# Two attentions of a transformer's last layer run as one sequence of 24 softmax steps, with the projections dealt out over it

## The chip, the cores and the metric

The kernel runs on one core of a Trainium2 chip. The metric is the device time of one execution in microseconds (us), as a median over runs. The engines are TensorE (PE in the rows; PEld is its weight load), VectorE (DVE), ScalarE (ACT), GpSimd (POOL, used only at the start) and SyncE (SP, which issues the loads of the weights). Each engine works through its own list of instructions in order, and the engines wait for each other by semaphores.

## The reference

The program computes four layers over 256 tokens of width 1024 in float32. The change touches the mixer of the last layer. There, with `h` the normalised input, `q` comes in 8 heads of 128 and `qm` in 4 heads of 128:

```python
proj = h @ b_w_q[j]                                  # 1024 x 1536
q  = proj[..., :1024].reshape(b, s, 8, 128)
qm = proj[..., 1024:].reshape(b, s, 4, 128)
# forgetting attention: causal, keys and values made before the layer's first feed-forward
logits = einsum('bqhd,bkhd->bhqk', q_blk, k) * scale + c_blk[..., :, None] - logf_cum[:, :, None, :]
p = softmax(where(causal, logits, NEG_INF));  y_tok = einsum('bhqk,bkhd->bqhd', p, v)
# memory attention: 256 memory positions, no mask
p = softmax(einsum('bshd,bmhd->bhsm', qm, mk) * dh ** -0.5);  y_mem = einsum('bhsm,bmhd->bshd', p, mv)
x = x + concatenate([y_tok, y_mem], -1) @ b_w_out[j]  # 1536 x 1024
```

## The kernel before

**Units.** The weights stream from HBM in units of 1 MB through a ring of three slots. A unit is loaded by SyncE into `raw`, ScalarE rounds it into `w_hi` (`split`, L1122), and VectorE makes the remainder `w_lo = raw - w_hi` (L1717). An *up* unit gives 256 columns of a projection from `normed` (L588 to L590: 8 pieces of k, each of 6 matmuls: two halves times hi by hi, hi by lo, lo by hi). A *down* unit takes 256 rows of an output projection and adds into all 1024 columns, which lie in PSUM banks 0 to 3 (L637 to L640: 8 column blocks `m`, each of 6 matmuls). When TensorE has finished a unit (`su_done`), ScalarE and then VectorE split the next contents of that slot; the slot's next load waits for VectorE's part (`lo_split`). The input of a down unit is prepared by `feed` (ScalarE L1220, VectorE L1827), which TensorE awaits as `hid_ready`.

**A softmax step** treats one head `h` and one half `a` of the queries (128 rows). Step n runs over the engines like this:
- TensorE, `scores(n)` (L830 for the last attention, called "fox"; L832 for the memory attention, "mem1"), issued two steps ahead: at the head of step n stands `scores(n+2)`. Then come `between(n)`, `values(n-1)` (L853) and `turn(n)` (L839), the transposes of the probabilities, which wait for `probs_ready(n)`.
- VectorE: `shift(n+1)` (the maximum, L2000; in fox an addition of the decays and the mask before it, L1994), `normalise(n)` (L2008, L2013), `between(n)`.
- ScalarE: `exps(n)` (L1318 or L1321), on odd n `copy_out` of a head (L1333), `copy_turned(n-1)` (L1328), `between(n)`.

`between` is where other work is woven in by hand. No planner orders it: the order of every engine is the order of this code.

**The stage around the change.** After the norm, TensorE does up units 0 and 1 (the memory queries), transposes the values, and does up unit 2. Then comes mem1, 8 steps, with up units 3 to 5 in halves (4 pieces of k a step) woven into its steps 0 to 5 (`B_WOVEN = 3`); its steps 6 and 7 have nothing between. Then TensorE waits until the last queries are evacuated and the last head is copied out, and fox begins, 16 steps, with down units 0 to 3 and a quarter of down unit 4 in quarters (two blocks `m`, 12 matmuls) woven in, three quarters ahead of step 1 by the table `FOX_DOWNS`. In fox a finished unit's slot is split whole, within the step that follows its last quarter, first by ScalarE and then by VectorE, in both queues ahead of the next step's softmax work. The rest of down unit 4, down unit 5 and the feed-forward follow. The mem1 scores use banks 0, 1 and 2 in turn and await nothing; the fox scores use banks 4 and 5 and await the `shift` of two steps before. Keys of a fox step are 128 for a = 0 and 256 for a = 1.

## Time and profile before

| what | us |
|---|---|
| median of 3 runs (1910.40 to 1911.62) | 1910.89 |
| the profiled execution's own time | 1911.35 |
| its span, first to last instruction | 1909.6 |
| TensorE busy in the span | 1830.5 (96%) |
| VectorE busy | 1353.2 (71%) |
| ScalarE busy | 1008.9 (53%) |
| the stretch from mem1's first scores to fox's last values | 1622.4 to 1700.4 |

Busy time of TensorE counts matmuls with their modelled ends, so back-to-back matmuls overlap in the rows; the time that a matmul costs is the distance from its start to the next start. In rows of the order of time, the figure in brackets is how long the engine was idle before, and what released it. The mean granted TensorE clock was 0.984 of full speed.

### The profile page before, as it was taken

How to read it: one execution, taken by the hardware profiler on the slowest of the kernel's cores; microseconds unless marked ns; L12 is line 12 of the kernel's file. 1: busy time of each engine (PE TensorE's matmuls, PEld its weight loads, DVE VectorE, ACT ScalarE, POOL GpSimd, SP SyncE). 2: the span in 40 equal slices, each digit the busy share in tenths (PEclk: the TensorE clock that was granted, in tenths of full speed). 3: DMA queues.
4: the chain of work that ended last, by engine and by line, in shares of the span. 5: the costliest groups of instructions: out<-in, count | busy, mean ns of one | idle time of the engine just before them, and what ended most of it. 6: DMA issues, size and time to landing. Idle time of an engine off the chain costs nothing.

```text
span 1909.6 us, 32527 instructions
## 1 busy us (share of the span) xinstructions
PE 1830.5 (96%) x12825; PEld 1700.1 (89%) x12825; DVE 1353.2 (71%) x1705; ACT 1008.9 (53%) x1205; POOL 5.3 (0%) x34
## 2 busy tenths in 40 slices
PE   6989899999999999999999999999999999899998
PEld 6988798998888889989999999999989999889997
DVE  5968668888788678886667666666756666666665
ACT  5744455566656555565445435444544445465443
POOL 1000000000000000000000000000000000000000
PEclk9999999999999999999999999999999999999999
DMA  6632155555533345556555554655645555336552
GB/s 187 189 121 89 50 172 176 177 197 182 172 116 133 112 167 172 187 166 208 178 179 175 172 177 155 198 177 176 198 134 203 180 188 167 121 101 209 176 178 85
DMA packets 237941, 310.18 MB, mean 162 GB/s; under 512 B 8227, under 2 KB 213801, under 8 KB 237865
## 3 DMA queue, kind: packets, MB, share of 16 engines
q1 hardware_dynamic: 236520, 308.03, 48.7%
q10 hardware_dynamic: 1344, 1.09, 0.2%
q8 instruction: 54, 0.88, 0.2%
q14 instruction: 23, 0.18, 0.0%
HBM read 308.04 MB, written 1.06 MB: 162 GB/s over the span
## 4 chain that ended last, share of the span: by engine, by line
PE 85%; DVE 8%; ACT 4%; issue 3%; DMA 0%; SPq 0%; DVEq 0%; ACTq 0%
PE ps L609 23%; PE ps L611 12%; PE ps L637 9%; PE ps L639 9%; PE ps L640 9%; PE ps L588 6%; PE ps L590 6%; PE ps L589 6%; DVE weights_lo L1717 2%; ACT weights_hi L1122 2%; PE ps L853 1%; DVE scratch L1767 1%; DVE scratch L1763 1%; ACT scratch L1245 1%; PE ps L756 1%
## 5 line engine op out<-in xcount | busy, mean ns | idle before, releaser
L1717 DVE TENSOR_TENSOR weights_lo<-raw_weights,weights_hi 128x2048 fp32r<-128x2048 f32 x290 | 663.9, 2290 | 260.6 <-ACT weights_hi L1122 260.1
L609 PE MATMUL ps<-normed,weights_hi 128*128 128x512 f32 x2112 | 749.3, 399 | 2.5 <-DVE normed L1807 2.4
L1122 ACT ACTIVATE weights_hi<-raw_weights 128x2048 fp32r<-128x2048 f32 x290 | 552.0, 1906 | 207.2 <-PE ps L590 84.5
L611 PE MATMUL ps<-normed,weights_lo 128*128 128x256 f32 x2112 | 593.1, 281 | 0.0
L609 PEld LDWEIGHTS ps<-normed,weights_hi 128*128 128x128 f32 x2112 | 396.9, 188 | 97.8 <-DVE weights_lo L1717 2.7
L637 PE MATMUL ps<-down_in_hi,weights_hi 128*128 128x256 f32 x1440 | 415.6, 289 | 18.9 <-DVE down_in_lo L1827 7.0
L639 PE MATMUL ps<-down_in_lo,weights_hi 128*128 128x256 f32 x1440 | 412.2, 286 | 0.0
L640 PE MATMUL ps<-down_in_hi,weights_lo 128*128 128x256 f32 x1440 | 411.9, 286 | 0.0
L611 PEld LDWEIGHTS ps<-normed,weights_lo 128*128 128x128 f32 x2112 | 399.2, 189 | 0.1
L588 PE MATMUL ps<-normed,weights_hi 128*128 128x256 f32 x1088 | 321.8, 296 | 10.7 <-DVE normed L1807 7.3
L589 PE MATMUL ps<-normed,weights_hi 128*128 128x256 f32 x1088 | 310.4, 285 | 0.0
L590 PE MATMUL ps<-normed,weights_lo 128*128 128x256 f32 x1088 | 310.4, 285 | 0.0
L637 PEld LDWEIGHTS ps<-down_in_hi,weights_hi 128*128 128x128 f32 x1440 | 281.2, 195 | 24.0 <-issue 13.7
L639 PEld LDWEIGHTS ps<-down_in_lo,weights_hi 128*128 128x128 f32 x1440 | 281.3, 195 | 0.2
L640 PEld LDWEIGHTS ps<-down_in_hi,weights_lo 128*128 128x128 f32 x1440 | 281.1, 195 | 0.0
L588 PEld LDWEIGHTS ps<-normed,weights_hi 128*128 128x128 f32 x1088 | 211.4, 194 | 15.3 <-issue 10.9
L589 PEld LDWEIGHTS ps<-normed,weights_hi 128*128 128x128 f32 x1088 | 211.4, 194 | 3.3 <-issue 2.6
L590 PEld LDWEIGHTS ps<-normed,weights_lo 128*128 128x128 f32 x1088 | 211.2, 194 | 0.0
L1191 ACT ACTIVATE scratch<-ps 128x512 f32<-128x512 f32 x132 | 78.3, 594 | 176.7 <-PE ps L611 176.7
L1763 DVE TENSOR_TENSOR scratch<-ps,scratch 128x512 f32<-128x512 f32 x132 | 90.7, 687 | 50.7 <-ACT scratch L1191 50.7
L1864 DVE SCALAR_TENSOR_TENSOR scratch<-scratch,vectors 128x254 f32<-128x254 f32 (+1 forms) x176 | 73.4, 479 | 60.9 <-ACT scratch L1245 60.9
L1245 ACT ACTIVATE scratch<-scratch,vectors 128x256 f32<-128x256 f32 x88 | 48.1, 594 | 116.8 <-DVE scratch L1767 116.8
(248 smaller groups left out, 1310.0 us busy)
## 6 DMA issues: line engine op xcount, KB each, us to landing
raw_weights<-in_ffn_w_gate_up_dram SPq DMA_DIRECT2D x88, 1024.0 KB, 5.1
raw_weights<-in_ffn_up_w_dram SPq DMA_DIRECT2D x44, 1024.0 KB, 5.1
raw_weights<-in_ffn_w_down_dram SPq DMA_DIRECT2D x44, 1024.0 KB, 5.0
raw_weights<-in_ffn_down_w_dram SPq DMA_DIRECT2D x22, 1024.0 KB, 4.9
raw_weights<-in_ssd_in_w_dram SPq DMA_DIRECT2D x20, 1024.0 KB, 5.3
raw_weights<-in_a_w_in_dram SPq DMA_DIRECT2D x14, 1024.0 KB, 5.1
raw_weights<-in_attn_in_w_dram SPq DMA_DIRECT2D x12, 1024.0 KB, 5.1
raw_weights<-in_ssd_out_w_dram SPq DMA_DIRECT2D x8, 1024.0 KB, 4.9
```

Source lines behind the costliest of these rows:

```text
L588: mm(o, hi, h_hi[:, k, :], start=(k == 0 and a == 0), stop=False, skip_group_check=True)
L589: mm(o, hi, h_lo[:, k, :], start=False, stop=False, skip_group_check=True)
L590: last = mm(o, lo, h_hi[:, k, :], start=False, stop=(k == DK - 1), skip_group_check=True)
L609: mm(ps[:, b + a, :], wh[:, k, a * P:(a + 1) * P], h[:, k, :, :].rearrange("p c t -> p (c t)"), start=(k == 0), stop=False, skip_group_che ...
L611: last = mm(ps[:, b + a, 0:T], wl[:, k, a * P:(a + 1) * P], h_hi[:, k, :], start=False, stop=(k == DK - 1), skip_group_check=True)
L637: mm(o, hi, act_hi[:, s, k, :], start=(first and k == 0 and m % 2 == 0), stop=False, skip_group_check=True)
L639: mm(o, hi, act_lo[:, s, k, :], start=False, stop=False, skip_group_check=True)
L640: ins = mm(o, lo, act_hi[:, s, k, :], start=False, stop=(k == 1), skip_group_check=True)
L1122: f(w_hi[:, s, :], raw[:, s, :], ACT.Copy).then_inc(hi_split.sem, hi_split.plus())
L1191: f(f_in[:, w, :, :], low_part(b), ACT.Copy).then_inc(low_copied.sem, low_copied.plus())
L1717: tt(w_lo[:, s, :], raw[:, s, :], f32(w_hi[:, s, :]), ALU.subtract).then_inc(lo_split.sem, lo_split.plus())
L1763: tt(f_in[:, w, :, :], main_part(b), f_in[:, w, :, :], ALU.add).then_inc(step.sem, step.plus())
```

## The change

Mem1 and fox become one sequence of 24 steps (8 and 16) without a wait between them. Only PSUM banks 4 and 5 hold scores now, in both kinds, bank 6 the transposes, bank 7 the values. So the scores of step n+2 await `exps` of step n where step n is of mem1 (it reads the bank directly), and `shift(n)` where it is of fox. The up units lie in banks 0, 1, 2, 1, 2, 0. Up units 3 to 5 are dealt out over steps 0 to 10 in pieces of 3, 3 and then 2 k a step. Down units 0 to 2 and the first quarter of down unit 3 are dealt out over steps 11 to 23, a quarter a step, with the blocks in reverse order; three quarters of unit 3 and units 4 and 5 follow the sequence. The order of the inputs is heads of mem1 first, then fox (`MIXED_ORDER`). A slot freed by the unit that ends in step t is split in halves of 1024 columns: ScalarE in steps t+1 and t+2, VectorE in steps t+3 and t+4. The two key masks of each half move from steps 0 to 3 to steps 1 and 4.

```diff
-B_WOVEN = 3
-FOX_PIECES = [(i, 2 * q) for i in range(5) for q in range(4)]
-FOX_DOWNS = {0: FOX_PIECES[0:2], **{t: FOX_PIECES[t + 1:t + 2] for t in range(1, 16)}}
-FOX_FED = {5: 0, 9: 1, 13: 2}
+MIXED_ORDER = (4, 5, 0, 1, 2, 3)
+JOINT_UPS = (3, 3, 2, 2, 2, 2, 2, 2, 2, 2, 2)
+JOINT_ENDS = {-1: ("up", 2), 2: ("up", 3), 6: ("up", 4), 10: ("up", 5), 14: ("down", 0), 18: ("down", 1), 22: ("down", 2)}
+JOINT_FED = {6: 0, 10: 1, 14: 2, 18: 3, 22: 4, 24: 5}
+JOINT_UP_BANKS = (0, 1, 2, 1, 2, 0)
+JOINT_KEYS = {1: (0, 1), 4: (2, 3)}
...
+        def score_bank(kind, n):
+            return 4 + n % 2 if joint(kind) else n % 3
...
                 def scores(n):
+                    kind, h, a = steps[n]
+                    b, nk = score_bank(kind, n), keys_of(kind, a)
+                    if joint(kind) and n >= 2:
+                        if steps[n - 2][0] == "fox":
+                            pe.wait_ge(shifted.sem, shifted.value(n - 1))
+                        else:
+                            pe.wait_ge(exps_done.sem, exps_done.value(n - 1))
...
-            softmax_attention("mem1", woven(B_WOVEN))
-            pe.wait_ge(evacuated.sem, evacuated.value())
-            pe.wait_ge(out_read.sem, out_read.value(1))
...
+            def joint_step(t):
+                if t < len(JOINT_UPS):
+                    query_parts(t)
+                else:
+                    quarter = t - len(JOINT_UPS)
+                    out_quarter(quarter // 4, quarter % 4)
+
+            softmax_attention(("mem1", "fox"), joint_step)
+            for q in range(1, 4):
+                out_quarter(3, q)
+            down_unit()
             down_unit(last=True)
...
+            def joint_step(t):
+                if t - 1 in JOINT_ENDS:
+                    act.wait_ge(su_done.sem, su_done.next())
+                    split_part(0)
+                if t - 2 in JOINT_ENDS:
+                    split_part(1)
+                    if JOINT_ENDS[t - 2][0] == "up":
+                        act.wait_ge(evacuated.sem, evacuated.next())
+                if t in JOINT_FED:
+                    act.wait_ge(out_read.sem, out_read.value())
+                    feed(mixed, MIXED_ORDER[JOINT_FED[t]], (out_slot + JOINT_FED[t]) % RING)
...
+            def split_part(part):
+                s, half = slot[0], slice(1024 * part, 1024 * part + 1024)
+                if part == 0:
+                    dve.wait_ge(hi_split.sem, hi_split.next())
+                ins = tt(w_lo[:, s, half], raw[:, s, half], f32(w_hi[:, s, half]), ALU.subtract)
...
+            def joint_step(t):   
+                if t - 1 in JOINT_ENDS:
+                    dve.wait_ge(su_done.sem, su_done.next())
+                    kind, j = JOINT_ENDS[t - 1]
+                    if kind == "up":
+                        last_queries(j - 2, None)
+                if t in JOINT_FED:
+                    feed(mixed, MIXED_ORDER[JOINT_FED[t]], (out_slot + JOINT_FED[t]) % RING)
+                for part in (0, 1):
+                    if t - 3 - part in JOINT_ENDS:
+                        split_part(part)
+                if t == 1:
                     dve.wait_ge(keys_staged.sem, keys_staged.next(2))
...
+                for i in JOINT_KEYS.get(t, ()):
+                    mask_keys(i)
```

In TensorE's list before, between the last woven up unit and the first down unit, stand these rows (L853 values, L839 turns, L832 scores of mem1, L830 scores of fox, L637 the first matmul of a down unit):

```order
L590 MATMUL ps<-normed,weights_lo 128x256
L853 MATMUL ps<-scratch,mem_v 128x128 x2
L839 MATMUL ps<-ident,scratch 128x128 x2
L853 MATMUL ps<-scratch,mem_v 128x128 x2
L839 MATMUL ps<-ident,scratch 128x128 x2
L853 MATMUL ps<-scratch,mem_v 128x128 x2
L839 MATMUL ps<-ident,scratch 128x128 x2
L853 MATMUL ps<-scratch,mem_v 128x128 x2
L830 MATMUL ps<-proj 128x128
L830 MATMUL ps<-proj 128x256
L830 MATMUL ps<-proj 128x128
L637 MATMUL ps<-down_in_hi,weights_hi 128x256
```

Four values, three turns and three scores stand there with no unit between them. In the changed list the same place, the end of the memory heads, reads so (L869 values, L855 turns, L845 scores of fox, L602 to L604 the matmuls of an up unit, of which 12 stand in each step):

```order
L869 MATMUL ps<-scratch,mem_v 128x128 x2
L855 MATMUL ps<-ident,scratch 128x128 x2
L845 MATMUL ps<-proj 128x128
L602 MATMUL ps<-normed,weights_hi 128x256
L603 MATMUL ps<-normed,weights_hi 128x256
L604 MATMUL ps<-normed,weights_lo 128x256
...
L869 MATMUL ps<-scratch,mem_v 128x128 x2
L855 MATMUL ps<-ident,scratch 128x128 x2
L845 MATMUL ps<-proj 128x256
L602 MATMUL ps<-normed,weights_hi 128x256
```

Two pieces of an up unit now stand in every step there, and the first fox scores are in front of such a piece.

In VectorE's list of fox before, from one `shift` to the next but one (L1994 and L2000 `shift`, L2008 and L2013 `normalise`, L1717 the split of a slot):

```order
L1994 SCALAR_TENSOR_TENSOR scratch<-ps,columns,scratch 128x128
L2000 TENSOR_REDUCE scratch<-scratch 128x1
L2008 RECIPROCAL scratch<-scratch 128x1
L2013 TENSOR_SCALAR scratch<-scratch 128x256
L1717 TENSOR_TENSOR weights_lo<-raw_weights,weights_hi 128x2048
L1994 SCALAR_TENSOR_TENSOR scratch<-ps,columns,mem_k 128x256
L2000 TENSOR_REDUCE scratch<-scratch 128x1
L2008 RECIPROCAL scratch<-scratch 128x1
L2013 TENSOR_SCALAR scratch<-scratch 128x128
L1994 SCALAR_TENSOR_TENSOR scratch<-ps,columns,scratch 128x128
```

The whole split of 2048 columns stands ahead of the shift of a 256-key step. Now, around step 10, the first with both a `feed` and a half split (L1885 the feed, L1766 a half split, L2052 and L2058 `shift`, L2066 and L2071 `normalise`, L1836 the evacuation of the last queries):

```order
L2071 TENSOR_SCALAR scratch<-scratch 128x128
L1885 TENSOR_TENSOR down_in_lo<-proj,down_in_hi 128x512
L1766 TENSOR_TENSOR weights_lo<-raw_weights,weights_hi 128x1024
L2052 SCALAR_TENSOR_TENSOR scratch<-ps,columns,scratch 128x128
L2058 TENSOR_REDUCE scratch<-scratch 128x1
L2066 RECIPROCAL scratch<-scratch 128x1
L2071 TENSOR_SCALAR scratch<-scratch 128x256
L1836 SCALAR_TENSOR_TENSOR proj<-ps,rstd 128x512
L2052 SCALAR_TENSOR_TENSOR scratch<-ps,columns,mem_k 128x256
```

The feed and a half split of 1024 columns stand ahead of the shift of a 128-key step and the `normalise` of the 256-key step before it. The other half stands three steps later.

## Rows read from the trace of the kernel before

**Rows 1.** The page: busy time, share of the span and instructions of each engine.

```profile
PE 1830.5 (96%) x12825; PEld 1700.1 (89%) x12825; DVE 1353.2 (71%) x1705; ACT 1008.9 (53%) x1205; POOL 5.3 (0%) x34
```

**Rows 2.** Stretches: length, busy PE, PEld, DVE, ACT, POOL (instructions), PE clock, DMA share, GB/s.

```profile
1622.40:1646.00 23.60, 23.60 (x188) 23.18 (x188) 17.54 (x32) 11.17 (x24) 0.00 (x0) 1.00 0.50 169
1646.00:1656.00 10.00, 5.54 (x31) 3.97 (x29) 5.78 (x10) 5.60 (x12) 0.00 (x0) 0.82 0.48 178
1656.00:1659.30 3.30, 3.30 (x18) 3.30 (x17) 1.61 (x7) 0.60 (x2) 0.00 (x0) 0.51 0.23 89
1681.90:1692.70 10.80, 9.23 (x74) 8.94 (x74) 7.26 (x19) 5.83 (x17) 0.00 (x0) 1.00 0.29 96
1622.40:1700.40 78.00, 68.08 (x518) 64.94 (x518) 49.38 (x109) 39.03 (x96) 0.00 (x0) 0.96 0.35 119
```

**Rows 3.** Order of time, TensorE, one mem1 step: start, length, instruction, count.

```profile
1626.84 0.60 PE L832 MATMUL ps<-mem_k,proj 128*128 128x256 f32 x2
...
1630.13 0.61 PE L853 MATMUL ps<-scratch,mem_v 128*128 128x128 f32 x4
...
1630.58 0.38 PE L839 MATMUL ps<-ident,scratch 128*128 128x128 f32 x2
...
1630.80 0.60 PE L832 MATMUL ps<-mem_k,proj 128*128 128x256 f32 x2
```

**Rows 4.** Order of time, TensorE, from mem1 to fox.

```profile
1646.03 0.61 PE L853 MATMUL ps<-scratch,mem_v 128*128 128x128 f32 x4
...
1651.66 0.71 PE L853 MATMUL ps<-scratch,mem_v 128*128 128x128 f32 x4 [0.53 <-ACT scratch L1328]
...
1655.49 0.80 PE L830 MATMUL ps<-proj 128*128 128x128 f32 x2 [0.93 <-DVE scratch L2000]
...
1655.94 0.56 PE L637 MATMUL ps<-down_in_hi,weights_hi 128*128 128x256 f32 x1
...
1659.27 0.28 PE L637 MATMUL ps<-down_in_hi,weights_hi 128*128 128x256 f32 x1
```

**Rows 5.** Order of time, TensorE, in and after fox.

```profile
1668.93 0.60 PE L853 MATMUL ps<-scratch 128*128 128x128 f32 x4
...
1671.11 0.33 PE L839 MATMUL ps<-ident,scratch 128*128 128x128 f32 x1 [1.57 <-DVE scratch L2013]
...
1681.91 0.33 PE L839 MATMUL ps<-ident,scratch 128*128 128x128 f32 x1 [1.57 <-DVE scratch L2013]
...
1699.94 0.71 PE L853 MATMUL ps<-scratch 128*128 128x128 f32 x4 [0.73 <-ACT scratch L1328]
```

**Rows 6.** Order of time, ScalarE and VectorE, a whole split in fox.

```profile
1665.50 1.91 ACT L1122 ACTIVATE weights_hi<-raw_weights 128x2048 fp32r<-128x2048 f32 x1
...
1667.52 2.29 DVE L1717 TENSOR_TENSOR weights_lo<-raw_weights,weights_hi 128x2048 fp32r<-128x2048 f32 x1 [3.10 <-ACT weights_hi L1122]
```

**Rows 7.** Order of time, the three engines, the first mem1 steps.

```profile
1622.45 1.46 PE L832 MATMUL ps<-mem_k,proj 128*128 128x256 f32 x6
...
1623.08 0.86 DVE L2000 TENSOR_REDUCE scratch<-ps 128x1 f32<-128x256 f32 x2 [0.87 <-PE ps L832]
...
1623.91 0.19 ACT L1321 ACTIVATION_READ_ACCUMULATOR scratch<-ps,scratch 128x1 f32 x1
```

**Rows 8.** Groups by line and form, over the kernel: 1024 columns wide.

```profile
L1793 DVE TENSOR_TENSOR scratch<-scratch 128x1024 f32<-128x1024 f32 x11 | 13.4, 1221 | 1.3 <-ACT scratch L1204 1.2
...
L1421 ACT ACTIVATE proj<-proj 128x1024 f32<-128x1024 f32 x4 | 4.2, 1054 | 0.7 <-DVE proj L2156 0.7
```

**Rows 9.** Order of time, ScalarE and VectorE, a feed; then a shift and normalise.

```profile
1671.64 0.62 ACT L1220 ACTIVATE down_in_hi<-proj 128x512 fp32r<-128x512 f32 x1
...
1672.30 0.69 DVE L1827 TENSOR_TENSOR down_in_lo<-proj,down_in_hi 128x512 fp32r<-128x512 f32 x1 [0.21 <-ACT down_in_hi L1220]
...
1674.15 0.35 DVE L1994 SCALAR_TENSOR_TENSOR scratch<-ps,columns,scratch 128x128 f32<-128x128 f32 x1
...
1674.92 0.35 DVE L2013 TENSOR_SCALAR scratch<-scratch 128x256 f32<-128x256 f32 x1
```

More of the change, by code:

```diff
@@ L328, in attention, with joint, softmax_steps @@
                     "mem0": (MEM_HEADS, 24, 36, P ** -0.5), "mem1": (MEM_HEADS, 24, 36, P ** -0.5)}[kind]
+        def joint(kind):
+            return kind in ("mem1", "fox")
         def turned_bank(kind):
-            return 6 if kind == "fox" else 3
+            return 6 if joint(kind) else 3
+        def score_bank(kind, n):
+            return 4 + n % 2 if joint(kind) else n % 3
+        def softmax_steps(kinds):
+            return [(kind, h, a) for kind in kinds for h in range(attention(kind)[0]) for a in range(TH)]
         def keys_of(kind, a):
@@ L622, in woven, with down_unit @@
                 return step
-            def down_unit(first=False, last=False, ms=range(DK)):
+            def down_unit(first=False, last=False, ms=range(DK), begin=True, end=True):
                 s = slot[0]
-                if ms[0] == 0:
+                if begin:
                     pe.wait_ge(lo_split.sem, lo_split.next())
@@ L1117, in _ @@
             slot, unit = [0], [0]
+            def split_part(part):
+                s, half = slot[0], slice(1024 * part, 1024 * part + 1024)
+                if part == 0:
+                    act.wait_ge(landed[s].sem, landed[s].next())
+                ins = f(w_hi[:, s, half], raw[:, s, half], ACT.Copy)
+                if part:
+                    ins.then_inc(hi_split.sem, hi_split.plus())
+                    unit[0] += 1
+                    slot[0] = (s + 1) % RING
             def split(s):
@@ L2022, in softmax_attention @@
                 shift(0)
[L2023 to L2024 removed]
+                for n in range(len(steps)):
+                    if n + 1 < len(steps):
                         shift(n + 1)
@@ L2027, in softmax_attention @@
                     between(n)
-                for n in range(2 * n_heads, 2 * n_heads + 3):
+                for n in range(len(steps), len(steps) + 3):
                     between(n)
@@ L2376, in _ @@
-            softmax_attention("mem1", mem_step)
-            turned.n += 4
-            dve.wait_ge(out_read.sem, out_read.next(MEM_HEADS))
-            mixed = proj[:, 28:40, :]
-            for j in range(2):
-                feed(mixed, 4 + j, (slot[0] + j) % RING)
-            def fox_step(t):
-                if 0 < t <= 15 and FOX_DOWNS[t - 1][-1][1] == DK - 2:
-                    dve.wait_ge(su_done.sem, su_done.next())
-                    split_next()
-                if t in FOX_FED:
-                    feed(mixed, FOX_FED[t], (slot[0] + 1) % RING)
@@ L2390, in _, with mask_keys @@
-            softmax_attention("fox", fox_step)
-            dve.wait_ge(out_read.sem, out_read.next(FOX_HEADS))
-            feed(mixed, 3, (slot[0] + 1) % RING)
+            memory_queries = queries_to_proj(24, JOINT_UP_BANKS)
+            last_queries = queries_to_proj(16, JOINT_UP_BANKS[2:])
+            units(2, memory_queries, evacuated=1)
+            mixed, out_slot = proj[:, 28:40, :], (slot[0] + 1) % RING
+            def mask_keys(i):
+                rows_of = key_rows[i // 2]
+                if i % 2:
+                    tt(rows_of[:, :, P:T], rows_of[:, :, P:T], rows(causal_mask[:, P:T], 4),
+                       ALU.add).then_inc(step.sem, step.plus())
+                else:
+                    tt(first_rows[:, 2 * i:2 * i + 4, :], rows_of[:, :, 0:P], rows(causal_mask[:, P:T], 4),
+                       ALU.add).then_inc(step.sem, step.plus())
+                dve.wait_ge(step.sem, step.value())
```

163 lines of the change are left out of this document (77 added, 86 removed).

## The prediction

> **What bounds the kernel now.** I read the page first, for the shares: TensorE is busy in 96% of the span [rows 1], so a change can only pay where TensorE stands still or runs slow. Then I took the busy time in stretches of the part that the change touches, 1622.4 to 1700.4: 78.0 us, of which TensorE shows 68.1 busy and VectorE 49.4 [rows 2]. The clean part of mem1 has no gap. The 10 us after it hold only 5.5 us of TensorE work, the next 3.3 us run at a granted clock of 0.51 (the 1.2 GHz level), and in fox a period of 10.8 us holds 9.2 us of work [rows 2]. Last I went to the rows in order of time, to price each loss by the distance between starts.
>
> What a step costs when nothing waits: a mem1 step of before runs from 1626.84 to 1630.80, 3.96 us. Values take 1630.13 to 1630.58, 0.45; the turn 0.22 to 1630.80; so scores with 24 matmuls of projection take 3.29, and at 0.12 a matmul (2.88) the scores are 0.41 [rows 3]. A piece of 128 keys takes half of each.
>
> **What the change removes.** Four losses of TensorE in that stretch.
>
> (a) The seam between the attentions. From the values at 1646.03 to the first down matmul at 1655.94 are 9.91 us [rows 4]. The work in it is four values (1.80), three turns (0.66) and scores of 128, 256 and 128 keys (0.21 + 0.41 + 0.21): 3.3 us. 6.6 us are waits: chains from engine to engine with nothing woven in. In the changed list that work has two pieces of an up unit in every step (1.44 us). Removed: 6.6, if the chains fit under the cover, which is checked below.
>
> (b) The slow clock behind the seam. From 1655.94 to 1659.27 15 matmuls start, at 0.213 us each where 0.12 is normal [rows 4], at the clock of 0.51 [rows 2]. 3.33 less 15 x 0.12 and 0.1 for the entry from float32 work: 1.4 us, and it goes with the idle time before it.
>
> (c) Three waits of a turn in fox. The values begin at 1668.93 and cost 0.45; the turn starts at 1671.11 [rows 5]: 1.73 us. The same row stands at 1681.91, and a third 10.8 us on, at 1692.72: 5.2 us together. Their cause is a whole split in line: ScalarE's 1.91 us at 1665.50 and VectorE's 2.29 at 1667.52 run one after the other [rows 6], and the exponentials and shifts queue behind each.
>
> (d) The last values of the sequence start 0.73 us late behind the copy [rows 5]; the copy waited for a whole split of ScalarE. With half of it in front, the wait should be that of a chain with ScalarE free, as at 1651.66: 0.53 [rows 4]. Removed: 0.2.
>
> **What it adds.** (e) The scores of step 2 now wait for the exponentials of step 0. Before, six instructions of scores ran through from 1622.45 [rows 7]. Now two scores end at 1622.45 + 0.82 = 1623.27 and the third waits for the maximum (from 1623.08) and the exponential, whose accumulator is read at 1623.91 + 0.19 = 1624.10 [rows 7]. With the signal, TensorE goes on at about 1624.12: 0.85 us lost, with nothing before it to cover. The same kind of wait stands ahead of every later score, and is covered there as follows.
>
> (f) The halves. A 1024-column instruction takes 1.22 on VectorE and 1.05 on ScalarE [rows 8]; two of them against one whole, 2.29 and 1.91 [rows 6]: 0.15 and 0.2 more a split, seven splits: 1.1 and 1.4 us. They lie beside TensorE unless they are on a chain. The Trainium skill, "VectorE: DVE Perf Modes", section on the TRN2 errata, says that operations from SBUF pay a fixed extra per instruction, so that many small tiles pay it each time. The rows agree that it is there; whether it is paid in time depends on the chain.
>
> (g) Moves. Four quarters of a down unit (4 x 1.43 us) leave the sequence and run behind it, as much work as before. Queries, masks, feeds and splits are as many as before. ScalarE's feed and the loads of SyncE move earlier or later by steps; the tightest load is that of the slot that is freed last, and it has more than 10 us of down units ahead of its use, where a step moved it by one. I cost it at nothing.
>
> **Do the chains fit?** Without waits a mem1 step with two pieces is 0.41 + 1.44 + 0.45 + 0.22 = 2.52 us, and four fox steps are 10.80 - 1.73 = 9.07 us [rows 5], 2.2 for a = 0 and 2.3 for a = 1. All the work of VectorE in the stretch is 49.4 us [rows 2], plus 1.1 for the halves, in a stretch that shrinks to 78.0 - 12.2 less the four quarters, some 60 us, in which about 5 of that work (two splits) moves behind it: three quarters full. So it does not bind by its sum, but in one place by its order.
>
> Mem1, scores(n+2): at the head of step n TensorE wants exps(n). ScalarE may begin step n-1's copy when the turn is done; copy, half a split (1.05) and the exponential with its read take 0.2 + 0.3 + 0.95 + 0.65 = 2.1 us from the head of step n-1; the step lasts 2.52. It fits by 0.4. Values(n-1) need the copy only at 1.85 us: it fits by more than 1.
>
> Fox: the tight place is the step with a feed and a half split, t = 10, 14, 18, 22. Let F be TensorE's start of step t. Before, the turn of a 128-key step started at 1671.11, so F was 1671.22, and the feed began at 1671.64 [rows 9], F + 0.42; behind a 256-key step the copy is longer by an estimated 0.1: F + 0.52. VectorE's feed follows 0.66 later and takes 0.62 to the next start [rows 9]: F + 1.8. The half split takes 1.13 of the 1.22 to the next start: F + 2.93. Then stand shift(t+2) and normalise(t+1): 1674.15 to 1674.92 + 0.35, 1.12 us [rows 9]: F + 4.05. TensorE reaches turn(t+1) after a step of 2.2, and 0.41 + 1.43 + 0.22: F + 4.26. It fits by 0.2 us. That is less than I can read from the rows, so I put 0.3 us in all for those four places. With a whole split there it would not fit by 0.9. Everything else has half a microsecond or more.
>
> **The sum.** Removed 6.6 + 1.4 + 5.2 + 0.2 = 13.4; added 0.85 + 0.3 = 1.15; net 12.2. The profiled execution took 1911.35 us (its span 1909.6 and 1.75 around it), 0.46 above the median of the runs. 1911.35 - 12.2 = 1899.1; against the median, 1910.89 - 12.2 = 1898.7. I predict 1898.7.
>
> Bounds. The unknowns are the new waits. From below: no wait at all, also not at (e), gives 13.4, 1897.5; I add 1 us for what my starts cannot see, 1896.5. From above: the four tight places may each wait as long as a whole half split on VectorE, 1.2 us [rows 8], 4.9 in all; 1903.3.
>
> **The rivals.**
>
> Feed-bound fox. VectorE waits for ScalarE's feed, and the feed for the copy behind the turn, so a late turn makes the next one late. For it: the 0.2 us of margin, and the 0.21 us that VectorE already waits for the feed [rows 9]. Against it: it comes once in four steps, and the other three have slack to catch up. It gives 0.5 to 1.2 us at four places and the same, once, at step 6: 2.5 to 6 us, 1901 to 1904.5.
>
> Every fixed cost counts. By that page's rule on small tiles, if each half stood on the chain, (f) would cost its full 2.5 us: 1901.2. The rows speak against it: VectorE works 7.3 of the 10.8 us of a period [rows 2] and its half split stands three steps after the unit's end.
>
> The clock falls inside the sequence. The seam shows the price: 3.3 us at 0.51 cost 1.4 us. For it: the gap of 0.85 at the start and alternating small work. Against it: in fox before, three gaps of 1.57 us left the clock at 1.00 [rows 2, 5]. Two such falls would give 2.8 us, 1901.5. The Trainium skill, "TensorE: Matmul & The Clock Gate", section on PSUM-queue cycling, tells of a kernel whose small idles between groups of matmuls made the clock go back and forth; the rows of this stretch do not agree, with gaps and a clock of 1.00.
>
> Slower than before: two banks instead of three bind every step. The mechanism is the loop scores, maximum, exponential, scores over two steps. In the sequence a step may last (78.0 - 4 x 1.43) / 24 = 3.0 us before the time is as before, so the loop would have to take more than 6.0 us per two steps in all 24. Its parts are 0.6 from scores to maximum, 0.9 for a shift with its addition, 0.65 for the exponential, and, if both halves of a split and a feed always fell into it, 1.05 + 1.22 + 0.62: 5.0 us. For it: the waits are new and stand at the head of the step, ahead of the cover. At 6.5 us per loop the kernel is 6 us slower, 1917. It decides only if the rows' durations grow, and I see no reason.
>
> The change does nothing: the seam comes back behind the sequence, since the three quarters and two units run with idle partners. They run back to back before, too. 1910.9.
>
> **How the numbers follow.** Forecast (within 1.5 us of 1898.7) 0.62; feed-bound fox 0.18; fixed costs 0.06; clock 0.04; less than the forecast for reasons I do not see, but still faster, 0.03; no change 0.04; slower 0.03. The range 1896.3 to 1903.2 holds the first and most of the next three. About 0.2% (3.8 us) is what a measurement of this kernel can tell from no change. Faster by more than that 0.93, within it 0.04, slower 0.03.
>
> **What the profile after would show.** Right: from the last woven matmul of mem1 on, no gap between values and scores, a granted clock of 1.00 from the first to the last step, and one PE wait of about 0.85 us for ScalarE's exponential at the third scores. Steps of 2.5 us in mem1 with two pieces and four fox steps in 9.1 us. (c) is wrong if turns still wait for L2071; the place to look is turn 11, 15, 19, 23. (d) shows 0.5 before the last values. (a) is wrong if scores wait for the exponential in each mem1 step. If the stretch shrinks by 13 us and the time does not, the loss is in the feed-forward behind it, in its first three units.

## The result, and the profile after

| what | before | after |
|---|---|---|
| median of 3 runs | 1910.89 (1910.40 to 1911.62) | 1897.06 (1895.60 to 1897.52) |
| the profiled execution | 1911.35 | 1897.52 |
| its span | 1909.6 | 1895.6 |
| granted clock over the span | 0.984 | 0.987 |

The ratio of the runs is 0.992, with a 95% interval of 0.9903 to 0.9938: 11.8 to 18.5 us faster. Forecast were 1898.7 us, 12.2 us faster; measured are 13.8 by the medians.

First the page of the profile after, the line that answers to [rows 1]:

```profile
PE 1824.9 (96%) x12825; PEld 1697.4 (90%) x12825; DVE 1353.2 (71%) x1712; ACT 1008.5 (53%) x1212; POOL 5.3 (0%) x34
```

TensorE has as many instructions as before, VectorE and ScalarE have seven more each (the halves). To see where the time went, cut the execution at two rows of TensorE: the first memory scores, and the first wide matmul of the feed-forward behind the mixer. The rows of the profile after, in order of time (start, length, instruction; in brackets the idle time and its releaser):

```profile
1621.28 1.03 PE L847 MATMUL ps<-mem_k,proj 128*128 128x256 f32 x4
1622.99 0.70 PE L847 MATMUL ps<-mem_k,proj 128*128 128x256 f32 x2 [0.68 <-ACT scratch L1364]
...
1680.17 0.71 PE L869 MATMUL ps<-scratch 128*128 128x128 f32 x4 [0.47 <-ACT scratch L1372]
...
1696.54 0.40 PE L623 MATMUL ps<-normed,weights_hi 128*128 128x512 f32 x1
```

And the end of the same stretch in the profile of before; its beginning is 1622.45 [rows 7]:

```profile
1710.55 0.40 PE L609 MATMUL ps<-normed,weights_hi 128*128 128x512 f32 x1
```

| piece of the span | before | after | difference |
|---|---|---|---|
| start to first memory scores | 1622.45 | 1621.28 | -1.17 |
| the stretch (first memory scores to first wide matmul) | 88.10 | 75.26 | -12.84 |
| behind it | 199.05 | 199.06 | 0.0 |

The last row is the span less the two others, and the span is printed to 0.1 us: hundredths count there for nothing. The instructions of the first piece and of the last are the same in both kernels, in the same order on TensorE, VectorE and ScalarE. The change made the stretch 12.84 us shorter; the 1.17 us in front are another matter, for the experiments. In the stretch the profile after has just the two waits of TensorE shown above. The view of stretches (length, busy PE, PEld, DVE, ACT, POOL, then PE clock, DMA share, GB/s), after, answers to [rows 2]:

```profile
1621.30:1696.50 75.20, 74.05 (x602) 72.63 (x601) 55.24 (x124) 44.91 (x112) 0.00 (x0) 1.00 0.40 136
```

and of before, the same work:

```profile
1622.40:1710.50 88.10, 78.18 (x602) 75.04 (x602) 54.91 (x117) 44.24 (x105) 0.00 (x0) 0.96 0.35 117
```

The granted clock is now 1.00 throughout, and busy TensorE fell too, by 4.1 us: the matmuls at the lower level are gone, and with the waits the modelled ends that stand ahead of them. A memory step, as [rows 3] had it, and four fox steps, as [rows 5] had them; after, order of time, TensorE:

```profile
1631.45 0.38 PE L855 MATMUL ps<-ident,scratch 128*128 128x128 f32 x2
...
1633.99 0.38 PE L855 MATMUL ps<-ident,scratch 128*128 128x128 f32 x2
...
1650.73 0.27 PE L855 MATMUL ps<-ident,scratch 128*128 128x128 f32 x1
...
1659.74 0.27 PE L855 MATMUL ps<-ident,scratch 128*128 128x128 f32 x1
...
1668.76 0.27 PE L855 MATMUL ps<-ident,scratch 128*128 128x128 f32 x1
```

2.54 us for the memory step with two pieces (forecast 2.52), 9.01 and 9.02 for four fox steps (forecast 9.07).

The tight place, step 10, in all three engines, after. TensorE's step starts with L845 at F = 1648.63:

```profile
1648.63 0.39 PE L845 MATMUL ps<-proj 128*128 128x128 f32 x2
...
1649.11 0.62 ACT L1262 ACTIVATE down_in_hi<-proj 128x512 fp32r<-128x512 f32 x1
...
1649.77 0.69 DVE L1885 TENSOR_TENSOR down_in_lo<-proj,down_in_hi 128x512 fp32r<-128x512 f32 x1 [0.67 <-ACT down_in_hi L1262]
...
1650.38 1.22 DVE L1766 TENSOR_TENSOR weights_lo<-raw_weights,weights_hi 128x1024 fp32r<-128x1024 f32 x1
...
1651.51 0.34 DVE L2052 SCALAR_TENSOR_TENSOR scratch<-ps,columns,scratch 128x128 f32<-128x128 f32 x1
...
1652.28 0.35 DVE L2071 TENSOR_SCALAR scratch<-scratch 128x256 f32<-128x256 f32 x1
...
1652.92 0.38 PE L855 MATMUL ps<-ident,scratch 128*128 128x128 f32 x2
```

The `normalise` (L2071) is done at 1652.63, F + 4.00 (forecast F + 4.05), and the turn that needs it starts at F + 4.29 (forecast F + 4.26), without a wait: a margin of 0.29 us. (The half split in this step is the second of its slot. The first stands one step earlier, at 1646.64, and not three steps later.) This is how a fit is read: not from the busy share, but from the end of the last instruction of the chain to the start of what would wait for it.

### The profile page after: what moved, and what is told of

Read it like the earlier page. It is cut to its first block, busy times and chain, and to the rows that moved or that the text cites. A ratio compares the mean times of both kernels' runs of the same rounds, so it can differ in the third digit from the quotient of the medians.

```text
span 1895.6 us, 32539 instructions
## 1 busy us (share of the span) xinstructions
PE 1824.9 (96%) x12825; PEld 1697.4 (90%) x12825; DVE 1353.2 (71%) x1712; ACT 1008.5 (53%) x1212; POOL 5.3 (0%) x34
## 4 chain that ended last, share of the span: by engine, by line
PE 86%; DVE 8%; ACT 3%; issue 3%; DMA 0%; SPq 0%; DVEq 0%; ACTq 0%
PE ps L623 23%; PE ps L625 12%; PE ps L651 9%; PE ps L653 9%; PE ps L654 9%; PE ps L602 6%; PE ps L604 6%; PE ps L603 6%; DVE weights_lo L1775 2%; ACT weights_hi L1164 1%; PE ps L869 1%; DVE scratch L1825 1%; DVE scratch L1821 1%; ACT scratch L1287 1%; PE ps L770 1%
## 5 line engine op out<-in xcount | busy, mean ns | idle before, releaser
L1775 DVE TENSOR_TENSOR weights_lo<-raw_weights,weights_hi 128x2048 fp32r<-128x2048 f32 x283 | 647.9, 2290 | 250.3 <-ACT weights_hi L1164 249.7
L1164 ACT ACTIVATE weights_hi<-raw_weights 128x2048 fp32r<-128x2048 f32 x283 | 538.5, 1905 | 208.7 <-DVE scratch L1825 84.3
L602 PE MATMUL ps<-normed,weights_hi 128*128 128x256 f32 x1088 | 322.2, 296 | 10.9 <-DVE normed L1865 7.2
L604 PE MATMUL ps<-normed,weights_lo 128*128 128x256 f32 x1088 | 310.4, 285 | 0.0
L602 PEld LDWEIGHTS ps<-normed,weights_hi 128*128 128x128 f32 x1088 | 211.3, 194 | 15.3 <-issue 10.6
L604 PEld LDWEIGHTS ps<-normed,weights_lo 128*128 128x128 f32 x1088 | 211.2, 194 | 0.0
```

The costliest lines, as they stand in the source:

```text
L602: mm(o, hi, h_hi[:, k, :], start=(k == 0 and a == 0), stop=False, skip_group_check=True)
L604: last = mm(o, lo, h_hi[:, k, :], start=False, stop=(k == DK - 1), skip_group_check=True)
L1164: f(w_hi[:, s, :], raw[:, s, :], ACT.Copy).then_inc(hi_split.sem, hi_split.plus())
L1775: tt(w_lo[:, s, :], raw[:, s, :], f32(w_hi[:, s, :]), ALU.subtract).then_inc(lo_split.sem, lo_split.plus())
```

## The experiments

Each run is measured against the kernel before on the same chip. "Stretch" is cut as above; TensorE's waits are all those in the stretch, from the order of time.

**The kernel once more, five executions.** No edit.

> The changed kernel once more, against the kernel before, on another occasion. Theory (chance outside the change): the stretch from the first scores of the memory attention to the first matmul of the last feed-forward takes 75.3 us again (88.1 before) and what follows it 199.1, both within 0.2; the arrival at the stretch, where all instructions are those of before, moves by 1 us or more from one execution to the next with the places at which the granted clock is low. Median difference 12.8 us, give or take 1. Rival (something systematic beyond the stretch): the stretch is 12.8 us shorter, but the medians stand 14 to 15 us apart again, and the arrival is about 1.2 us earlier again.

Measured: median 1898.44 us of 5 (1896.82 to 1900.71), before 1911.88 of 11 (1908.59 to 1915.68); ratio 0.9932, interval 0.9918 to 0.9946, that is 13.0 us (10.3 to 15.7). The profile: arrival at the first memory scores 1621.86, stretch 75.26, behind it 199.08. The stretch repeats to the hundredth; the arrival does not.

**Is the arrival chance?** The kernel before once more, one profile.

> The kernel before, unchanged, one profile. Theory (the granted clock ahead of the stretch differs from one execution to the next, in the same instructions): the first memory scores start anywhere between 1620 and 1624.5 us and not at 1622.45 again, while the stretch is 88.1 and the rest to the end of the span 199.05, each within 0.1 us. Rival (the change itself, through the loads, moves the arrival earlier): the arrival is later here than in every profile of the changed kernels, 1622.4 or more, and the stretch or the rest may differ by more than 0.3.

Measured: arrival 1622.28, stretch 88.10, behind it 199.12; the time is 1911.18. Alone it does not decide, since 1622.28 is close to 1622.45. All profiles together say more: in kernels that are the same up to the first memory scores the arrival lies from 1620.17 to 1624.22 (table below), on both sides of before. The mean of eleven profiles of changed kernels is 1622.08, that of two of before 1622.37. Where the spread arises, the start of the same whole split on ScalarE shows in four of them (numbered in order of time):

| profile | 26th | 75th | 87th | 111th | 124th | arrival |
|---|---|---|---|---|---|---|
| before | 236.2 | 539.5 | 647.9 | 793.4 | 873.5 | 1622.45 |
| after | 235.7 | 538.9 | 645.3 | 790.6 | 871.5 | 1621.28 |
| third bank (below) | 234.1 | 537.4 | 645.8 | 791.2 | 871.3 | 1620.17 |
| whole with the feed (below) | 238.6 | 541.8 | 648.2 | 793.5 | 874.3 | 1624.22 |

From the 75th to the 87th two take 108.4 us and two 106.4; from the 111th to the 124th those with 108.4 take 80.1 and the others 80.8 or 80.9. The rows of the stretches there, before:

```profile
600.00:640.00 40.00, 33.92 (x227) 30.68 (x226) 23.22 (x46) 20.50 (x46) 0.00 (x0) 0.87 0.29 103
840.00:880.00 40.00, 37.58 (x252) 34.48 (x251) 31.58 (x38) 26.59 (x31) 0.00 (x0) 1.00 0.50 163
```

and after:

```profile
600.00:640.00 40.00, 33.74 (x244) 30.80 (x243) 24.92 (x46) 20.63 (x47) 0.00 (x0) 0.96 0.29 102
840.00:880.00 40.00, 37.91 (x238) 34.83 (x239) 30.90 (x35) 27.27 (x30) 0.00 (x0) 0.96 0.48 159
```

The third bank's profile has the clocks of before there (0.87, 1.00), the whole split with the feed those of after (0.96, 0.96), worth 2.0 and 0.8 us. These are not the only values: over all thirteen profiles the first window was granted 0.87 ten times, 0.91 once and 0.96 twice, the second 1.00 seven times, 0.96 four times and 0.91 twice, and the changed kernel has 0.96 and 0.96 in one of its two profiles, 0.87 and 1.00 in the other. The rest of the spread is there by the 26th split, 234.1 to 238.6; its cause was not read. So the arrival moves by itself, and no run ties the 1.17 us to the change; with two profiles of before, a shift of some tenths can't be told from none. Why a place is granted the lower level in one execution and not in the next, no run here shows.

**A third bank for the one scores that wait uncovered.** It undoes (e) alone.

```diff
-            return 4 + n % 2 if joint(kind) else n % 3
+            return (3 if n == 2 else 4 + n % 2) if joint(kind) else n % 3
-                    if joint(kind) and n >= 2:
+                    if joint(kind) and n >= 3:
```

> The third scores go to PSUM bank 3, which is free by then, and wait for nothing. Theory: the wait of TensorE for the exponential at the start goes, and nothing takes its place, so the stretch is 0.7 to 0.85 us shorter than 75.3, about 74.5. Rival (the wait only moves one step on, to the scores of step 3, as the exponential of step 1 queues behind half a split): less than 0.2 us.

Measured: stretch 74.32, 0.94 less; one execution, 1895.46 us. Only the wait of 0.47 before the last values is left. So (e) costs 0.94 us; the row shows 0.68 of it.

**A quarter of a down unit ahead of the last values.** It covers what (d) left.

```diff
-            softmax_attention(("mem1", "fox"), joint_step)
-            for q in range(1, 4):
+            softmax_attention(("mem1", "fox"), joint_step, before_last=lambda: out_quarter(3, 1))
+            for q in range(2, 4):
```

> The last values stand behind the next quarter of the down unit, not ahead of it. Theory: the wait of 0.47 us for the copy goes under 12 matmuls, the stretch is 0.5 us shorter, about 74.8. Rival: the last feed, which needs the last head copied out, comes 1.4 us later and holds up the last down unit: the stretch is as long or longer.

Measured: stretch 74.52, 0.74 less; one execution, 1895.92 us. The row showed 0.47. Again the wait costs a quarter of a microsecond more than its idle time. The rows say where it lies. First, idle time is counted from the modelled end of the matmul before, and that end is later than the next start has to be: in [rows 3] the turn at 1630.58 takes 0.38, to 1630.96, and the scores behind it start at 1630.80, 0.16 earlier. Second, the instruction behind a wait is longer itself: scores take 0.70 where they take 0.60 without a wait, values 0.71 for 0.61, a turn 0.33 for 0.27. So a wait costs its idle time and 0.26 us more ahead of scores or values, and 0.22 more ahead of a turn.

**Both.**

> Both edits (third scores in bank 3, last values behind a quarter). Theory: they add, since each takes away one wait of TensorE and leaves none: stretch 74.1 us (1.2 shorter), no wait of TensorE left in the sequence; the median 1.2 us under that of the changed kernel, which the rounds can hardly tell. Rival: one of them is only moved, 0.5 to 0.8.

Measured: stretch 73.57, 1.69 less, the sum of the two. Median 1897.37 of 6 (1896.09 to 1897.82, and one execution of 3581.61; 1897.00 without that one), before 1911.88; ratio 0.9924, interval 0.991 to 0.9937. So it was executed again, on another chip:

> The kernel with bank 3 for the scores of step 2 and a down quarter ahead of the last values, measured once more. Theory that what lies outside the stretch is chance: the stretch from the first scores to the first wide matmul of the feed-forward is 73.6 us (within 0.1) and TensorE waits nowhere in it; the median lies between 1896.0 and 1898.5 us, 13.5 to 15.5 below the kernel before of the same runs; no execution of 3582 us comes back. Rival, that the long execution belongs to this kernel: it comes again at least once in the six.

Measured: median 1896.23 of 5 (1895.20 to 1898.82), before 1911.2 of 9 (1909.29 to 1915.06); ratio 0.9923, interval 0.9909 to 0.9937: 14.7 us. Stretch 73.58. No long execution came back; where the 3581.61 came from stays open (its granted clock was 1.0). In this kernel TensorE is busy without a gap; two of its stretches, as the others:

```profile
1650.00:1660.00 10.00, 10.00 (x83) 9.85 (x82) 8.93 (x21) 6.59 (x20) 0.00 (x0) 1.00 0.31 107
1660.00:1670.00 10.00, 10.00 (x85) 9.90 (x84) 8.26 (x24) 7.01 (x19) 0.00 (x0) 1.00 0.32 107
```

That gives the measure for everything else: 73.57 us is the stretch with no wait at all. (The brackets alone don't prove it, as the last experiment shows. The distances from start to start do: none is longer than the same pair of instructions takes in the other steps of its kind.) The interval of the medians overlaps that of the changed kernel. That this kernel is the faster of the two rests on the stretch, which repeats to 0.01 us, and not on the medians.

**The seam, with the projection left in mem1.** Up units 3 to 5 in steps 0 to 5 as before, nothing between in steps 6 to 10; one sequence all the same.

```diff
-JOINT_UPS = (3, 3, 2, 2, 2, 2, 2, 2, 2, 2, 2)
+JOINT_UPS = (4, 4, 4, 4, 4, 4, 0, 0, 0, 0, 0)
-JOINT_ENDS = {-1: ("up", 2), 2: ("up", 3), 6: ("up", 4), 10: ("up", 5), ...}
+JOINT_ENDS = {-1: ("up", 2), 1: ("up", 3), 3: ("up", 4), 5: ("up", 5), ...}
```

> The up units stand in steps 0 to 5, 4 pieces a step, as before; steps 6 to 10 of the joint sequence have nothing between. Theory (uncovered steps are what the seam cost, not the two waits that separated the attentions): such a step takes 1.4 us where its work is 1.1 (memory) or 0.75 (last attention), more where a half split stands in the chain: 4 to 7 us in all, and if the granted clock falls in it, 1.4 more: stretch 79 to 84 us. Rival (the separating waits were the cost): under 2 us longer.

Measured: median 1907.37 of 10 (1904.93 to 1911.21), before 1910.31 of 13 (1908.94 to 1914.87); ratio 0.9981, interval 0.9971 to 0.9991. Stretch 84.92, 9.66 longer than in the changed kernel. TensorE's waits in the bare steps, order of time (a sixth, of 0.25, is at 1654.40):

```profile
1649.12 0.71 PE L869 MATMUL ps<-scratch,mem_v 128*128 128x128 f32 x4 [0.25 <-ACT scratch L1372]
...
1651.04 0.70 PE L845 MATMUL ps<-proj 128*128 128x256 f32 x2 [0.99 <-ACT scratch L1364]
...
1653.49 0.44 PE L855 MATMUL ps<-ident,scratch 128*128 128x128 f32 x2 [1.12 <-DVE scratch L2071]
...
1655.86 0.33 PE L855 MATMUL ps<-ident,scratch 128*128 128x128 f32 x1 [0.75 <-DVE scratch L2071]
...
1658.09 0.69 PE L855 MATMUL ps<-ident,scratch 128*128 128x128 f32 x2 [0.98 <-DVE scratch L2071]
```

and its stretches:

```profile
1650.00:1660.00 10.00, 5.84 (x27) 4.05 (x27) 9.14 (x20) 5.81 (x18) 0.00 (x0) 0.89 0.32 107
1660.00:1670.00 10.00, 10.00 (x65) 9.48 (x64) 5.53 (x20) 3.94 (x15) 0.00 (x0) 0.77 0.30 107
1670.00:1680.00 10.00, 10.00 (x85) 9.90 (x84) 7.02 (x19) 6.91 (x20) 0.00 (x0) 1.00 0.01 2
```

Joining the two attentions gives nothing by itself. The stretch is 3.18 us shorter than before (84.92 for 88.10), but no turn waits behind the bare steps here, so that the 5.37 us of (c) and 0.26 of (d) (both measured below) are gained and 0.94 of (e) is paid, 4.69 in all: the bare seam costs 1.5 us more than the old one with its separating waits. Cover in every step gives the 9.66. In the bare steps VectorE binds (9.14 of 10 us): the steps are short, and four half splits of 1.22 us fall into steps 6 to 9, one in each. No run has bare steps without these splits, so what part of the 9.66 us is theirs and what part the missing cover's, is not shown. The granted clock falls in the last bare steps (0.50 from 1658 to 1662) and is 0.77 over these ten us, much as at the old seam [rows 2, 4], and 1.00 again in the next ten. The 9.66 us are more than the 5.4 to 8.4 that I had given it: I had priced chains of waits, and not that VectorE's half splits fall into the bare steps.

**A whole split in line, in fox.** It undoes (c) for the down units.

```diff
 # ScalarE
-                    split_part(0)
-                if t - 2 in JOINT_ENDS:
+                    if JOINT_ENDS[t - 1][0] == "up":
+                        split_part(0)
+                    else:
+                        split_next()
+                if t - 2 in JOINT_ENDS and JOINT_ENDS[t - 2][0] == "up":
...
 # VectorE, under "if t - 1 in JOINT_ENDS"
+                    else:
+                        split_next()
...
-                    if t - 3 - part in JOINT_ENDS:
+                    if t - 3 - part in JOINT_ENDS and JOINT_ENDS[t - 3 - part][0] == "up":
```

> For the down units the two engines split whole in step t+1, one behind the other, as the last attention did before; the up units' slots in halves as in the changed kernel. Theory: the waits of 1.7 us come back at the turns of steps 16 and 20; the one behind step 22 has only the last turn behind it, and the last values then wait 0.3 to 2 us more: the stretch is 3.5 to 5.5 us longer, about 80. Rival (the waits of before came from the seam's rhythm and not from the serial split): under 1 us longer.

Measured: median 1901.99 of 4 (1900.54 to 1902.00), before 1910.31; ratio 0.9953, interval 0.9936 to 0.9969. Stretch 79.10, 3.84 longer. The old waits come back with their old length [rows 5]:

```profile
1666.78 0.33 PE L855 MATMUL ps<-ident,scratch 128*128 128x128 f32 x1 [1.57 <-DVE scratch L2075]
...
1677.59 0.33 PE L855 MATMUL ps<-ident,scratch 128*128 128x128 f32 x1 [1.57 <-DVE scratch L2075]
...
1684.81 0.71 PE L869 MATMUL ps<-scratch 128*128 128x128 f32 x4 [0.73 <-ACT scratch L1372]
```

The last wait is 0.26 longer than in the changed kernel (0.73 for 0.47), and 3.84 - 0.26 = 3.58 is 1.79 us for each of the other two.

**Halved, or only moved? A whole split with the feed.** VectorE's split stands whole at step t+4, the step of the feed.

```diff
-                for part in (0, 1):
-                    if t - 3 - part in JOINT_ENDS:
-                        split_part(part)
+                if t - 4 in JOINT_ENDS:
+                    split_next()
```

> VectorE splits a slot whole in step t+4 (the step that also has a feed); ScalarE still in halves. Theory (the tight place is the one with feed and split, margin 0.27 us in the changed kernel's trace): 1.07 us more of VectorE in front makes the turn of steps 11, 15 and 19 late by 0.8 us each, that of step 7 by 0.2; step 23 has no shift behind it and waits 0.2 at most: the stretch is 2.4 to 2.9 us longer, about 78. Rival (there is slack of a whole step, the halves buy nothing): under 0.5 us longer.

Measured: median 1902.98 of 4 (1901.24 to 1904.61), before 1910.31; ratio 0.9957, interval 0.9941 to 0.9974. Stretch 79.44, 4.18 longer, where I had expected 2.4 to 2.9. The tight place, all three engines, to be read beside step 10 above:

```profile
1663.76 2.28 DVE L1775 TENSOR_TENSOR weights_lo<-raw_weights,weights_hi 128x2048 fp32r<-128x2048 f32 x1
...
1665.97 0.34 DVE L2052 SCALAR_TENSOR_TENSOR scratch<-ps,columns,scratch 128x128 f32<-128x128 f32 x1
...
1666.73 0.35 DVE L2071 TENSOR_SCALAR scratch<-scratch 128x256 f32<-128x256 f32 x1
...
1667.14 0.44 PE L855 MATMUL ps<-ident,scratch 128*128 128x128 f32 x2 [0.67 <-DVE scratch L2071]
```

The same turn waits after each feed: 0.33 at 1647.34, 0.67 three times, and 0.74 at 1686.36, which I had put at 0.2 or less. 3.1 us idle at five places cost 4.18: 0.22 more for each, the price of a wait ahead of a turn.

**Whole, but one step earlier.** No halves at all: ScalarE whole in step t+1, VectorE whole in step t+3, where no feed stands.

```diff
-                    split_part(0)
+                    split_next()
...
-                for part in (0, 1):
-                    if t - 3 - part in JOINT_ENDS:
-                        split_part(part)
+                if t - 3 in JOINT_ENDS:
+                    split_next()
```

> No halves at all: ScalarE splits whole in step t+1, VectorE whole in step t+3, ahead of the feed step. Theory (the place of VectorE's split matters, not its halving): VectorE is done with it before the feed comes, and the turns in fox do not wait; ScalarE's whole split delays the exponential of step 4, for which the scores of step 6 wait, by 0.4 us: the stretch is 0 to 0.6 us longer than 75.3. Rival (halving is what took the waits of fox away): 1.5 us or more at each of four places, 81 us.

Measured: median 1898.89 of 4 (1898.64 to 1901.69), before 1910.31; ratio 0.9943, interval 0.9926 to 0.996. Stretch 76.03, 0.77 longer. No turn waits in fox. Two waits are new or longer, both for ScalarE, one at memory scores (0.25 + 0.26 = 0.51) and one before the last values (0.26 more):

```profile
1635.57 0.70 PE L847 MATMUL ps<-mem_k,proj 128*128 128x256 f32 x2 [0.25 <-ACT scratch L1364]
...
1681.89 0.71 PE L869 MATMUL ps<-scratch 128*128 128x128 f32 x4 [0.73 <-ACT scratch L1372]
```

**Whole splits in the kernel without waits.** Both edits of "both", and these.

> Bank 3 and the quarter ahead of the last values, and every slot split whole: ScalarE one step after the unit's end, VectorE three steps after it. If place counts and halving hardly does: the stretch is 73.6 plus the one wait of 0.25 us in mem1 that the whole split on ScalarE made, so 73.8 to 74.1 (the last values wait no longer, since a quarter stands ahead of them), median 1896.5 to 1899. If the halves are needed once TensorE waits nowhere else: new waits of a turn at steps 11, 15 or 19, 0.5 us or more each, 75 or more.

Measured: median 1898.35 of 4 (1895.00 to 1899.59), before 1911.2; ratio 0.9925, interval 0.9908 to 0.9942. Stretch 74.49, 0.92 longer than without any wait, where I had expected 0.2 to 0.5. One wait of 0.25 is shown, and by the distance from turn to turn it costs 0.51 (3.05 for 2.54). The other 0.41 is at the first step: the turns stand at 1626.66 and 1630.32, 3.66 apart where the halves gave 3.25, and no bracket shows it:

```profile
1626.66 0.38 PE L855 MATMUL ps<-ident,scratch 128*128 128x128 f32 x2
...
1626.93 0.20 ACT L1365 ACTIVATION_READ_ACCUMULATOR scratch<-ps,scratch 128x1 f32 x1
...
1627.18 0.70 PE L847 MATMUL ps<-mem_k,proj 128*128 128x256 f32 x2
```

The scores could start at 1626.88 and start at 1627.18, right behind ScalarE's read, which ends at 1627.13: 0.30 late, and they take 0.70 for 0.60, together the 0.41. TensorE's modelled end of the turn, 1627.04, fills more than half of the 0.30, and the rest, 0.14, was too short for a bracket. So halves are worth 0.8 to 0.9 us, and every wait that comes without them is for ScalarE; what VectorE needs is a place away from the feed. A kernel with halves on ScalarE and a whole split on VectorE at step t+3 was not run.

All profiles, by the same three cuts ("behind" is good to 0.05, for the span is printed to 0.1); "waits" are the idle times in brackets, summed:

| kernel | arrival | stretch | behind | waits |
|---|---|---|---|---|
| before | 1622.45 | 88.10 | 199.05 | 9.9 |
| before, again | 1622.28 | 88.10 | 199.12 | 9.9 |
| after | 1621.28 | 75.26 | 199.06 | 1.15 |
| after, again | 1621.86 | 75.26 | 199.08 | 1.15 |
| third bank | 1620.17 | 74.32 | 199.11 | 0.47 |
| quarter at the end | 1620.45 | 74.52 | 199.03 | 0.68 |
| both | 1622.38 | 73.57 | 199.05 | 0 |
| both, again | 1621.71 | 73.58 | 199.11 | 0 |
| bare steps | 1623.29 | 84.92 | 199.49 | 5.5 |
| split in line | 1622.08 | 79.10 | 199.12 | 4.55 |
| whole with the feed | 1624.22 | 79.44 | 199.04 | 4.23 |
| whole, step t+3 | 1622.23 | 76.03 | 199.04 | 1.66 |
| both, whole | 1623.22 | 74.49 | 199.39 | 0.25 |

## Why the prediction came out as it did

The mechanism was right, and the time fell in the range, but outside the band of 1.5 us around the forecast: the median is 1.64 us below 1898.7. The stretch lost 12.84 us for 12.2 forecast. The other 1.0 us lies outside the stretch, which no term of the sum had looked at; in the profiled executions it is the arrival, 1.17 us earlier. By terms, with 73.57 us as the stretch without waits:

- **(a) and (b), the seam and its clock**: forecast 6.6 + 1.4 = 8.0. Before lost 88.10 - 73.57 = 14.53 in all; less (c) 5.37 and 1.00 for the last values that leaves 8.16. What of it is clock and what is wait, no run parts. That it goes with cover in every step, the waits of the profile after show: none is left there.
- **(c), the three turns**: forecast 5.2. Measured 1.79 each, 5.37 together: from the split in line, and from four fox steps in 10.80 before and 9.01 after. I had read 1.73 from the row, which leaves out 0.06: the turn behind the wait is longer too.
- **(d), the last values**: forecast 0.2 removed, from 0.73 to 0.53. The row went from 0.73 to 0.47, and in time from 1.00 (0.73 and the 0.26 that such a wait costs besides) to 0.74: 0.26.
- **(e), the scores of step 2**: forecast 0.85, measured 0.94. It is the price of the two banks at the one place without cover. With 2.54 us of work between them, the later scores of mem1 wait nowhere.
- **The allowance of 0.3 at the four tight places**: not needed. The chain took F + 4.00 for F + 4.05 and the turn came at F + 4.29 for F + 4.26. The sentence beside it, that a whole split there would not fit by 0.9, is borne out: 0.67 idle, and 0.2 more in time.
- **(f), the halves' fixed cost**: the fourteen half splits took 1218 ns on VectorE and 1055 on ScalarE, within 3 ns of [rows 8], and are beside TensorE. Their cost was put too high even on their own engines: I had compared durations, but an instruction starts before the one ahead of it ends. From start to next start two halves take 2.27 us on VectorE and 1.90 on ScalarE, a whole split 2.21 and 1.81: 0.06 and 0.09 more a split, not 0.15 and 0.2. Busy VectorE in the stretch rose by 0.33 us (54.91 to 55.24). The time shows none of it.
- **(g), the moves**: nothing, right. The piece behind the stretch is 199.06 for 199.05.

Sum: 8.16 + 5.37 + 0.26 - 0.94 = 12.85, against 12.84 measured between the cuts. That it closes is no proof, since 8.16 is what was left over. What supports the seam's price is that this remainder agrees with the 8.0 worked out from the rows of before.

**The step that failed** is the last of the sum, "against the median, 1910.89 - 12.2 = 1898.7", with the band of 1.5 us around it. It takes all that lies outside the stretch as a constant, a term of nothing with no reason given. Measured, the medians stand 1.0 us further apart than the stretches. In thirteen profiles the 1622 us ahead of the change spread over 4 us, of which 2.0 and 0.8 us lie at two places where the granted clock differs, and the runs of before spread over 7 (1908.59 to 1915.68). The terms inside the stretch were short too, by 0.64 us together: 0.3 for the allowance, which was put on waits that did not come, 0.17 in (c), 0.16 in (a) and (b), 0.06 in (d), less 0.09 in (e), and the rest rounding. And the chances have no line for a gain larger than the band. On which side of the band a median falls is in part luck: the second set of five gave 1898.44, inside it.

The bound from below has the same fault. It lies 2.4 us below the forecast and is worked out from the new waits alone, which is less than the same instructions scatter: one of the three first executions, 1895.60, lies below it. Its "no wait at all, also not at (e), gives 13.4" was also no such thing, for it left the last values a wait of 0.53; the kernel without any wait gave 14.53. By the scatter, an honest low end was some 2 us lower, as an estimate. Last, I priced (d) by the idle time in the brackets and (a) and (c) by the distance between starts. The latter is what counts.

**The rivals.** The feed-bound fox did not come: no turn waits. It was near, as the whole split with the feed shows at just these places, with 4.18 us. That every fixed cost counts (the Trainium skill, "VectorE: DVE Perf Modes", on the errata) did not come either; the fixed part is in the rows, and not in the time. The clock inside the sequence stayed at 1.00 over 75 us of transposes, values, scores and matmuls in turn, with idle times of 0.68 and 0.47, and in the split in line waits of 1.57, 1.57 and 0.73 us left it at 1.00 too. What the Trainium skill tells in "TensorE: Matmul & The Clock Gate", on PSUM-queue cycling, of small idles that make the clock go back and forth, has no case in the changed kernel. The bare steps are nearer to it: six waits of 0.25 to 1.12 us within 10 us, and a granted clock of 0.50 behind them, though once and not back and forth. The two banks bind once, not in every step. Nothing speaks for no change.

## What to carry to other kernels

When two stages of small, dependent steps stand one behind the other, it is not the joining that pays but a piece of independent work in every step: joined and bare, the seam of this sequence was 1.5 us dearer than with the two attentions apart, and covered it left TensorE no wait. Before halving an instruction that blocks a queue, try another place for it: moved one step away from the feed it cost 0.8 us whole, next to the feed 4.2. And price a wait by the distance between starts on the engine that waits, then look at the same cut in several executions before a range is given.

## What the runs showed of the hardware

- A wait of TensorE costs more than its idle time in the rows: 0.68 idle cost 0.94, 0.47 cost 0.74, 0.25 cost 0.51, 1.57 cost 1.79, 3.1 at five places 4.18. About 0.16 us of it is the modelled end of the matmul before, which the next start need not await; the rest is a longer first instruction (0.70 for 0.60, 0.33 for 0.27). A short wait shows no idle time at all, and one such cost 0.41.
- On VectorE and ScalarE an instruction starts before the one ahead of it ends, so durations add up to more than the time they take in a queue: two half splits of 1.22 us take 2.27 on VectorE, one whole of 2.29 takes 2.21.
- The same instructions reach the same row at 1620.17 to 1624.22 us in thirteen executions; at 600 to 640 us the granted clock was 0.87, 0.91 or 0.96 among them (0.87 for 0.96 cost 2.0 us), at 840 to 880 us 1.00, 0.96 or 0.91 (0.96 for 1.00 cost 0.8). Behind the stretch the piece of 199 us repeated to 0.1 us, but for two kernels (199.39 and 199.49), whose granted clock in it was also the lowest, 0.982 and 0.981, for 0.984 to 0.989 in the others.
- One execution of 3581.61 us, at 1895.2 to 1898.8 in all ten others of that kernel, did not come back.
